# Two weight units loaded in four blocks each, and the last residual store moved ahead, beside the routing of a mixture-of-experts layer

## What is computed

```python
x = x + mix @ p['w_out']                 # the residual rows, x2 in the kernel
t = _rmsnorm(x, p['norm2_g'])            # hn2 in the kernel
gl = t @ w_router_group + b              # best of 4 groups
el = t @ w_router_expert + b             # best 2 of 8 experts in it
for e in range(32):
    a = t @ p['w_gate'][e]
    u = t @ p['w_up'][e]
    out = out + combine[:, e:e + 1] * ((jax.nn.silu(a) * u) @ p['w_down'][e])
y = _rmsnorm(x + out, final_norm_g)
```

## Time and profile before

| | us |
|---|---|
| median of 3 runs | 736.8 |
| their range | 736.21 to 737.12 |
| the profiled execution's own time | 734.72 |
| its span from first to last instruction | 733.0 |
| mean granted PE clock, share of full speed | 0.982 |

### The profile page before, as it was taken

One profiled execution on the slowest core, in us unless ns is written; L12 is line 12 of the kernel. 1 busy time (PEld: TensorE's weight loads), 2 busy tenths in 40 slices (PEclk: granted clock), 3 DMA queues, 4 the chain that ended last, 5 costly groups with the idle time before them and its releaser, 6 DMA issues.

```text
span 733.0 us, 9145 instructions
## 1 busy us (share of the span) xinstructions
PE 652.5 (89%) x3164; PEld 314.2 (43%) x3164; DVE 251.0 (34%) x516; ACT 161.5 (22%) x317; POOL 95.4 (13%) x161
## 2 busy tenths in 40 slices
PE   8999999999998899996899999877878776778995
PEld 4478888874455533332233333322222222223331
DVE  7798997187266520101010111100000100001057
ACT  3677511232432111110011111101000101001033
POOL 5100000000000212122012122211211112111000
PEclk9999999999999899997899999999999999999998
DMA  9533005469736899999999999999999999999983
GB/s 326 218 115 114 3 1 203 170 256 430 284 118 258 323 412 425 426 421 421 429 426 424 425 425 421 424 423 427 424 424 426 427 424 425 427 424 423 417 344 121
DMA packets 30004, 246.52 MB, mean 336 GB/s; under 512 B 6064, under 2 KB 6576, under 8 KB 16896
## 3 DMA queue, kind: packets, MB, share of 16 engines
q1 hardware_dynamic: 23216, 233.95, 77.1%
q0 software_dynamic: 5280, 8.21, 3.1%
q10 hardware_dynamic: 1456, 3.62, 1.3%
HBM read 235.65 MB, written 19.20 MB: 348 GB/s over the span
## 4 chain that ended last, share of the span: by engine, by line
PE 48%; DMA 36%; DVE 10%; ACT 3%; issue 2%; SPq 0%; POOLq 0%; POOL 0%; DVEq 0%
PE psA L1407 25%; DMA mem<-in_w_gu 25%; PE psB L1407 21%; DMA mem<-in_w_down 7%; DVE mem L731 4%; DMA mem<-hn_d,mem 2%; DVE mem L955 1%; DMA mem<-in_w_vb 1%; ACT front_c L665 1%; DMA hn_d<-front_c 1%; DVE mem L870 1%; ACT mem L673 1%; DVE mem L882 1%; PE psA L1412 1%; DVE mem L912 1%
## 5 line engine op out<-in xcount | busy, mean ns | idle before, releaser
L1407 PE MATMUL psA<-mem 128*64 128x512 f32 (+8 forms) x1368 | 309.0, 515 | 26.5 <-DMA mem<-in_w_gu 16.4
L1407 PE MATMUL psB<-mem 128*64 128x512 f32 (+7 forms) x1210 | 267.1, 540 | 31.6 <-DMA mem<-in_w_gu 20.3
L1407 PEld LDWEIGHTS psA<-mem 128*64 128x64 f32 (+4 forms) x1368 | 142.3, 151 | 174.4 <-issue 126.3
L1407 PEld LDWEIGHTS psB<-mem 128*64 128x64 f32 (+3 forms) x1210 | 109.0, 152 | 172.5 <-issue 123.0
L731 DVE TENSOR_TENSOR mem<-mem 128x512 f32<-128x512 f32 (+17 forms) x116 | 67.6, 597 | 23.7 <-ACT mem L565 19.6
L1163 DVE TENSOR_TENSOR front_c<-front_c,psA 64x512 f32<-64x512 f32 x15 | 10.3, 690 | 175.8 <-ACT front_c L665 175.8
L1163 DVE TENSOR_TENSOR front_c<-front_c,psB 64x512 f32<-64x512 f32 x15 | 10.3, 690 | 171.3 <-ACT front_c L665 171.3
L1325 POOL DMA_INDIRECT y_d<-front_c,mem x30 | 30.8, 1028 | 268.3 <-ACT front_c L676 268.3
L1320 POOL DMA_INDIRECT mem<-hn_d,mem x34 | 36.0, 1058 | 94.6 <-DMA hn_d<-front_c 65.4
L665 ACT ACTIVATE front_c<-psA 64x512 f32<-64x512 f32 x15 | 8.8, 589 | 121.6 <-PE psA L1407 121.6
L665 ACT ACTIVATE front_c<-psB 64x512 f32<-64x512 f32 x15 | 8.8, 589 | 115.3 <-PE psB L1407 115.3
(11 more groups left out here) (246 smaller groups left out, 365.3 us busy)
## 6 DMA issues: line engine op xcount, KB each, us to landing
mem<-in_w_gu SPq DMA_DIRECT2D x63, 2048.0 KB, 33.4
mem<-in_w_down SPq DMA_DIRECT2D x31, 2048.0 KB, 37.6
mem<-in_w_out SPq DMA_DIRECT2D x2, 2048.0 KB, 8.4
y_d<-mem SPq DMA_DIRECT2D x1, 4096.0 KB, 11.8
mem<-y_d SPq DMA_DIRECT2D x8, 512.0 KB, 8.4
mem<-in_x_T SPq DMA_DIRECT2D x8, 260.0 KB, 8.8
mem<-in_w_vb SPq DMA_DIRECT2D x8, 256.0 KB, 8.9
mem<-in_x_prompt SPq DMA_DIRECT2D x4, 512.0 KB, 11.2
```

What stands on the lines that cost most here:

```text
L1407: return nc.tensor.matmul(out, lhsT, rhs, start=start, stop=stop, skip_group_check=True)
```

## The change

Unit 7 and unit 9 are each loaded by four DMAs of 512 KB, with runs of 4 KB, in place of one of 2 MB with runs of 16 KB. The store of the last x2 rows is issued right behind unit 7 and no longer waits for the landing of the hn2 stores. In place of that wait, unit 9 waits for `hn2_rdy` (ACT has read x2 and written hn2) and, as before, for the landing of the x2 stores. `PRIOR` only corrects the counts that PE waits for, since each block adds its own 16 to the slot's semaphore.

```diff
-        PRIOR = {6: 2, 7: 3}
+        PRIOR = {6: 2, 7: 3 + 3, 9: 3}
...
+            def load_by_blocks(q):
+
+                e, j = UNITS[q]
+                s = q % NSLOT
+                for k in range(4):
+                    block = slice(2 * DE * k, 2 * DE * k + 2 * DE)
+                    unit(s, (ring[:, s, block], (w_dn[e] if j == 2 else w_gu[2 * e + j])[:, block]))
...
             sp.wait_ge(o_ps, NT + 1)
-            load(7)
-            sp.wait_ge(hn2_out[0], 48)
-            sp.wait_ge(hn2_out[1], 32)
+            load_by_blocks(7)
             store_x2(NT - 1)
             sp.wait_ge(x2_out, 16 * NT)
-            load(9)
+            sp.wait_ge(hn2_rdy, NT)
+            load_by_blocks(9)
```

## The result

| | before | after |
|---|---|---|
| median, us | 736.55 (4 runs) | 742.31 (4 runs) |
| range, us | 736.21 to 737.12 | 741.13 to 742.88 |
| span of the profiled execution, us | 733.0 | 739.4 |

The changed kernel is slower by 5.8 us: recorded ratio 1.0072, 95% interval 1.0049 to 1.0094 (the two medians of the table alone give 1.0078). The forecast was 736.5, with a range up to 739.2; the measured time lies above it.

A forecast was written before the change was run, and what follows sets the result against it. The prediction held that the weight stream bounds the kernel, so its start sets the end. Unit 10's earlier start -0.9, faster small pieces -0.2 and gather 0's delay +0.8 gave -0.3 us: median 736.5, range 735.7 to 738.2, widened to 739.2.

The forecast's parts named there:

- What bounds the kernel: Experts' weight stream, full at 425 GB/s from 264 to 660 us; PE waits, so the stream's start sets the end.
- Step 1: Before the experts: x2 store lands at 237.3 to 239, so unit 9 is issued 2.3 to 4 us earlier.
- Step 2: Start of unit 10: its first piece finds a free queue, gaining 0.9 us; the DMA engines idle in between.
- Step 3: Unit 10's two small first pieces, in 4 KB runs, move faster without the mix of queues: 0.2 us gained.
- Step 4: Last hn2 store lands at 235.8 to 238.7, or 1 us more; gather 0 issued at 238.9.
- the 239.6 named as a sign of being wrong: The prediction is wrong if the last hn2 store lands after 239.6.
- Step 5: Gather 0, beside unit 9's blocks, takes 5.2 us and lands at 244.1; cost taken as 0.8 us.
- The floor of 243.14: Before expert 0, PE's dummies run until it turns the rows at 243.14; an earlier gather 0 brings nothing.
- Rival 2: Gather 0 is caught behind unit 9's blocks for 7.3 to 8.66 us: 738.8 to 740.1; chance 0.26.
- Rival 1: Gather 0 gets through the small blocks within 4.2 us, PE keeps its start: 734.9 to 735.7; chance 0.22.
- Rival 3: x2 store lands at 240 or later, unit 9 starts within 1.3 us of its old time: 736.4; chance 0.10.
- that is PE's time and not the stream's, and is worth nothing: Halfway through expert 0: PE's idle 1.32 us for gather 1 should go, with no gain at the end.

The follow-up runs named there:

- e3: Changed kernel plus 24 more dummy products of PE before it waits for gather 0: 738.91 us, ratio 1.003.
- e5b: Kernel before with units 7 and 9 in blocks, the x2 store ahead of unit 7, unit 9 waiting for x2_out and hn2_rdy: 739.04 us, ratio 1.0035.
- e1: Kernel before with units 7 and 9 in four blocks of 4 KB runs, old order and waits: 734.87 us, ratio 0.9976.
- e10: The kernel of e1 measured once more in the second set: 734.59 us, ratio 0.9981.
- e11: e10 with unit 7 held back until the last hn2 store is under way: 738.88 us, ratio 1.0035.
- e8: Kernel before with unit 9 alone in four blocks, unit 7 left whole: 734.98 us, ratio 0.9987.
- e7: Changed kernel with two of unit 9's blocks (1 MB) issued ahead of gather 0, the rest after its landing: 738.48 us, ratio 1.0034.
- e4: Changed kernel with all four of unit 9's blocks waiting for gather 0's landing: 736.86 us, ratio 1.0003.

## Why the prediction was wrong

**What bounds the kernel: right.** In the earlier trace rows and after, 264 to 660 us run at 425 GB/s. In the traces the end follows the start of the stream: in e3 unit 10's first piece comes 5.5 us later behind unit 7 than before, some 4.5 of it behind the 248.1 at which unit 9 had made way, and the traced execution ends 4.6 us later behind unit 7.

**Step 1, unit 9 earlier: right in kind, too optimistic.** I had the x2 store landing between 237.3 and 239, 8.9 to 10.7 us behind unit 7's issue of 228.31. Unit 9 was issued 11.87 us behind it in the changed kernel (239.57 - 227.70), 12.98 before. It came 1.1 us earlier, not 2.3 to 4. That was enough to bring it ahead of gather 0, which itself came 1.3 us later.

**Step 2, the gain is small because the engines idle afterwards: right.** The gap is there, 0 and 12 GB/s from 248 to 252. e5b shows the limit: 6.8 us earlier, nothing won. The gain of 0.9 us itself can't be seen apart, as the first piece was late in every run with the new order.

**Step 3, the pace of the small pieces: of no weight.** They were paced by PE. The price that the prediction gave the smaller blocks did not show either: with blocks and the old order the kernel was not slower (e1, e10).

**Step 4, the hn2 store: the term mis-sized.** I let the smaller runs help it (3.1 to 6.0 us, with 1 us more only as an aside) and took gather 0's issue at 238.9. Run size did nothing: 6.09 us beside blocks in e1 against 5.96 beside long runs. The bytes ahead did: nothing 2.6 us (e11), unit 7 5.96 to 6.2, unit 7 and the x2 store 7.3 to 8.1. It cost 1.3 us. Moved by the 0.6 us by which this execution is ahead, the store lands at 240.0, past the 239.6 named as a sign of being wrong, and gather 0 is issued at 240.9, outside the bounds of 238.65 to 240.5.

**Step 5, gather 0's landing: the step that failed.** I interpolated by the size of the competing runs, 3.1 and 7.3 us to 5.2, and took 0.8 us of delay from it. The quantity to use was how many bytes stand ahead of the gather when POOL has written it. In the kernel before, gather 0 had almost none, since unit 9 was held until 241.29 by the x2 store, which was held by the hn2 landing. The prediction's remark that the first of unit 9's bytes may come behind gather 0's had the order the wrong way round. The removed wait did useful work: it kept 2 MB behind the gather. Gather 0 took 7.16 us, 4.1 more.

**What was left out: PE's clock behind an idle gap.** I had read the granted clock of 0.50 under the dummies and drew nothing from it. The floor of 243.14 itself hangs on it: in e1 and e8, with the clock at 1.00 there, the dummies were over at 242.2 and 242.0 and PE waited 0.46 and 0.60 us for gather 0. The dummies, by my own floor of 243.14, cover only 5 us; a gather that comes later leaves PE idle, and then expert 0 starts at the lower level. From the turning of the rows to unit 10's first piece passed 4.34 us instead of 2.92, and e3, which takes the idle gap away and leaves gather 0 late, gives back 3.4 us of 5.8.

The account, from unit 7's issue to unit 10's first piece: hn2 +1.3, gather 0 +4.1, less the 0.4 us by which PE's dummies had outlasted gather 0 before, PE's lower clock +1.4, together 6.4 us, as measured. Since unit 10's bytes had to wait for unit 9 until 248.1 before, the stream starts some 5.3 us late, and more is lost between 252 and 262, at 98 to 336 GB/s. Over the whole stretch from 228 to 264 us the engines moved 319 GB/s before and 246 after, 2.6 MB less, which is 6.2 us of the stream at 425 GB/s.

**Rival 2 was what happened**, with 0.26, and its price of 738.8 to 740.1 was too low, as it lacked the clock and took hn2's store as unharmed. Its point of decision, 6.9 us for gather 0, was passed. **Rival 1** rested in part on the rule of the Trainium skill (DMA: Bandwidth & Descriptors, Queues, rings and completion order) that an engine switches between queues after some 9 to 17 descriptors. The runs do not bear it out here. From 242 to 244 us of the changed kernel, with the gather written by 241.6, the engines moved only packets of SP's queue, and from 244 to 246 mostly these still:

```profile
q1 hardware_dynamic: 219, 0.81, 101.8%
...
q1 hardware_dynamic: 193, 0.69, 87.8%
q0 software_dynamic: 34, 0.11, 13.4%
```

The first row is 14 packets per engine, which the rule would allow; the two together are 26 per engine, with the gather having moved 34 of its packets in all. It took 7.16 us where the rule had given 4.3, and the wait kept growing from 1 to 2 MB ahead (e7, changed kernel). The measurement decides. **Rival 3** had its condition come true and its conclusion fail: unit 9 started within 1.3 us of its old time (1.1 us earlier), but gather 0 did not go as before, since the order of the two had turned.

**One sentence against me on the other side**: "that is PE's time and not the stream's, and is worth nothing", of PE's idle 1.32 us for gather 1. e1 and e10 took this gap away and had medians 1.8 to 1.9 us lower, with the stream at 432 instead of 391 GB/s behind it in e10. At this point PE still paces the stream, since only it gives slots back, so the sentence gave a wrong reason; how much of the medians' gain comes from here is open, as said at e10.

## What to carry to other kernels

Before a bulk load is moved ahead of a small transfer, count the bytes that will stand ahead of that transfer when it is issued, on every queue; here 2 MB ahead cost a gather 4 us, whether in runs of 4 or of 16 KB. Ask also whether the move turns the order of two transfers around; here 1.1 us of lead for the one and 1.3 us of delay for the other were enough. A wait that looks like mere tidiness may be what keeps the bulk behind the small transfer. And where the bulk cannot be consumed earlier anyway, since the slot behind it comes free later, moving it ahead has a price and no gain. Idle PE time in front of a stage costs twice if the clock falls in it, so dummies should last as long as the latest arrival they are to cover.

## What the runs showed of the hardware

- A small DMA on one queue waits for what other queues have been given before it. The store of 0.5 MB from ACT's queue: 2.6 us with nothing ahead, 6.0 to 6.2 behind 2 MB of SP's, 7.3 to 8.1 behind 2.5 MB. A part of these had moved when the store was issued: by the packets moved until then, 0.9 MB were left in the kernel before and 1.6 MB in the changed one. The gather on POOL's queue: 3.1 to 3.2, 4.26, 4.80 and 7.16 us with 0, 0.5, 1 and 2 MB ahead.
- This does not go on without limit. In the experts' loop a load lands 47 us behind its issue, so some ten units are queued, and yet a gather takes 8.8 us there in the median:

```profile
DMA to landing us min/median/max: 2.9/8.8/10.5
```

  (the row of the scratch tensor hn_d in the changed kernel, over all its DMAs). Over the 3.1 us of a gather alone that is 5.7 us, by the 425 GB/s of the stream an estimated 2.4 MB, little more than one unit. What sets this limit was not tried.
- Blocks mattered in one place only: gather 1, written about when unit 9 was issued, took 8.66 us beside one DMA with runs of 16 KB and 6.1 to 6.3 beside four with runs of 4 KB (e1, e8, e10). This need not be the size of the runs. Gather 1 was written at 242.12 before, behind all of unit 9 (241.29); in e10 it was written at 241.99, while SP was still issuing the four blocks (241.15 to 242.90), so that fewer bytes stood ahead of it. No run tried this apart.
- The PE clock's fall is not the same in every execution: the granted clock in 236 to 242 us was 0.50 in e10 and 1.00 in e1 and e8, with the same instructions. In eight traces PE had stood idle in front of expert 0 for 2.08 to 5.88 us, and in each of them it fell during or behind the gap: 5.74 us idle and 0.50 from 244 to 254 in the changed kernel, 2.90 us idle and 0.50 from 246 to 252 in e4, 3.68 us idle and 0.50 from 248 to 250 in e5b, 2.08 us idle and 0.50 from 246 to 252 in e11. In e3, idle for 1.57 us, and in e1 and e8, idle for 0.46 and 0.60 us, it stayed at 1.00.

The best version found is that of e1 and e10: blocks for units 7 and 9 with the old order and waits, 734.6 to 734.9 us, ratio 0.9981 (0.9964 to 0.9998) against the kernel before.
